# An eight-core decoder-layer kernel: the gating bias moves from TensorE to VectorE, value tiles are tracked one by one, the last normalised writes of a stage move into the next stage, and the last squares go to TensorE directly

## What is computed

```python
def rmsnorm(x, g):
    y = xf * lax.rsqrt(jnp.mean(xf * xf, axis=-1, keepdims=True) + EPS); return y * g
# layer 0
h = rmsnorm(x, norm_mix[0]); z = h @ w_in_even
x = x + concat(pool_mixer(z), conv_mixer(z)) @ w_out_even
x = x + swiglu(rmsnorm(x, norm_ffn[0]))        # (silu(h@Wg) * (h@Wu)) @ Wd, D_FF 2816
# layer 1
z = gelu(rmsnorm(x, norm_mix[1]) @ w_in_odd);  u, v = split(z)
v = rmsnorm(v, g_v)
mixed = einsum('hts,bnshd->bnthd', tril(w_s), chunks_of_128(v)) + b_s   # bias per head and position
x = x + (u * mixed) @ w_out_odd
x = x + swiglu(rmsnorm(x, norm_ffn[1]))
y = rmsnorm(x, norm_final)
```

## Time and profile before

| | |
|---|---|
| median of three runs | 1371.45 us (1371.28 to 1371.82) |
| the profiled execution: its time / its span | 1371.84 us / 1370.3 us (core 2) |
| spans of the eight cores | 1367.2 to 1370.3 us, mean granted clock 0.984 to 0.985 |
| PE busy | 1307.4 us (95%) |
| PEld, DVE, ACT, POOL busy | 721.8, 652.1, 348.3, 214.1 us |

### The profile page before, as it was taken

The page is one execution under the profiler, slowest core; times in us unless marked ns, Lnnn a source line. Parts: engine busy times, 40 slices in busy tenths (PEclk is TensorE's granted clock), DMA queues, the critical chain, the costliest instruction groups (busy, mean ns, idle before and its releaser), DMA issues.

```text
span 1370.3 us, 21873 instructions; the slowest of 8 cores (1367.2 to 1370.3 us)
## 1 busy us (share of the span) xinstructions
PE 1307.4 (95%) x7406; PEld 721.8 (53%) x7406; DVE 652.1 (48%) x1146; ACT 348.3 (25%) x673; POOL 214.1 (16%) x247
## 2 busy tenths in 40 slices
PE   4998997999999999999999999999999999999993
PEld 2554544555555655565444565555565555555552
DVE  3887477223526235632853335822272542644265
ACT  3423342111010110012556324411101011011164
POOL 3200262000000000001821004600000000000076
PEclk9999998999999999999999999999999999999998
DMA  9524203112211223103060101041113111220105
GB/s 264 114 38 63 48 1 62 32 31 54 41 31 32 39 55 62 32 16 61 3 108 1 34 1 32 5 89 32 31 36 58 32 32 31 55 39 16 32 32 217
DMA packets 11048, 68.16 MB, mean 50 GB/s; under 512 B 2056, under 2 KB 2186, under 8 KB 4780
## 3 DMA queue, kind: packets, MB, share of 16 engines
q0 software_dynamic: 6912, 47.19, 19.6%
q1 hardware_dynamic: 3452, 18.95, 3.9%
q10 hardware_dynamic: 576, 0.62, 0.1%
HBM read 105.32 MB, written 9.18 MB: 84 GB/s over the span
## 4 chain that ended last, share of the span: by engine, by line
PE 84%; DVE 7%; issue 4%; POOL 2%; ACT 2%; DMA 1%; DVEq 0%; SPq 0%; ACTq 0%; POOLq 0%
PE bank L741 57%; PE bank L812 16%; PE bank L836 4%; PE bank L1146 2%; PE bank L973 2%; DMA xTs<-xT 1%; POOL sqall L628 1%; DVE R L1168 1%; PE bank L894 1%; DVE hTs L668 1%; DVE R L1088 1%; DVE R L1085 1%; PE bank L1207 0%; PE bank L1199 0%; POOL rsv L1165 0%
## 5 line engine op out<-in xcount | busy, mean ns | idle before, releaser
L741 PE MATMUL bank<-hTs,wring 128*128 128x512 bf16 (+2 forms) x4160 | 737.1, 339 | 12.6 <-DVE mix L794 8.6
L741 PEld LDWEIGHTS bank<-hTs,wring 128*128 128x128 bf16 x4160 | 406.8, 98 | 333.3 <-issue 21.1
L794 DVE TENSOR_TENSOR mix<-bank,gtmp 128x512 bf16<-128x512 f32 (+2 forms) x220 | 129.2, 588 | 472.7 <-PE bank L741 470.4
L749 DVE TENSOR_TENSOR xTs<-bank,xTs 128x512 f32<-128x512 f32 (+2 forms) x480 | 278.9, 587 | 93.8 <-PE bank L741 32.7
L791 ACT ACTIVATE gtmp<-bank 128x512 f32<-128x512 f32 (+2 forms) x220 | 112.8, 515 | 723.5 <-PE bank L741 701.3
L812 PE MATMUL bank<-mix,wring 128*128 128x512 bf16 (+2 forms) x1280 | 224.7, 338 | 0.0
L812 PEld LDWEIGHTS bank<-mix,wring 128*128 128x128 bf16 x1280 | 125.2, 98 | 98.2
L125 POOL DMA_DIRECT2D wring<-wts x46 | 25.0, 543 | 972.0 <-PE bank L741 451.8
L628 POOL TENSOR_TENSOR sqall<-sqall 128x512 f32<-128x512 f32 (+5 forms) x138 | 147.1, 1066 | 95.0 <-ACT sqall L624 82.6
L741 PE MATMUL bank<-mix,wring 128*128 128x512 bf16 (+2 forms) x640 | 113.2, 338 | 0.0
L624 ACT ACTIVATE sqall<-xTs 128x512 f32<-128x512 f32 (+2 forms) x138 | 75.3, 548 | 91.5 <-DVE xTs L749 70.6
(11 more groups left out here) (104 smaller groups left out, 466.1 us busy)
## 6 DMA issues: line engine op xcount, KB each, us to landing
wring<-wts POOLq DMA_DIRECT2D x38, 1024.0 KB, 9.1
xTs<-xT SPq DMA_DIRECT2D x3, 2048.0 KB, 24.1
yT<-xTs SPq DMA_DIRECT2D x3, 2048.0 KB, 6.4
wring<-wts POOLq DMA_DIRECT2D x4, 768.0 KB, 9.3
wring<-wts POOLq DMA_DIRECT2D x4, 512.0 KB, 7.8
mix<-wts POOLq DMA_DIRECT2D x2, 1024.0 KB, 18.6
xTs<-xT SPq DMA_DIRECT2D x1, 1088.0 KB, 34.6
xTs<-xT SPq DMA_DIRECT2D x4, 256.0 KB, 5.2
```

The costliest lines, as they stand in the source:

```text
L741: last = E.matmul(bk[:, 0:w], lhsT=wt[:, o:o + 128], rhs=src_[:, k, c0:c0 + w], start=(k == 0), stop=(k == nk - 1))
L749: sc.op("dve", lambda E: E.tensor_tensor(out=xs(m, n), in0=bk[:, 0:w], in1=xs(m, n), op=ALU.add), reads=[bkB, xB[m][n]], writes=[xB[m][n]])
L794: sc.op("dve", lambda E, bu_=bu_, gi=gi, w=w, c0=c0, slot=slot: E.tensor_tensor(out=mix[:, slot, c0:c0 + w], in0=bu_[:, 0:w], in1=gtmp[gi] ...
```

## The change

1. The bias matmuls of U are gone, with `bs2`, `bs02`, `sel` and their eight DVE operations in `late_setup`. The bias comes repeated over the 128 partitions by one DMA of 512 KB into `bsT` (the space of the squares), issued in V behind tile 1. DVE adds it in PSUM in f32 before its multiplication.
2. `ssB` becomes 17 buffers, one for each token tile.
3. `nm.end()` no longer empties the list, except in the last norm; `last` puts the norm on `active`, and `drip` pops three entries behind each Silu product of `ffn_up`, or two for each token tile of V. `use_banks(8)` comes when the list is empty.
4. The squares of the blocks in `direct` are written by ACT in bf16 into buffers of their own and summed by ones matmuls of their own, for every n: block 7 in the norms behind `out0` and `out1`, blocks 6 and 7 behind both `ffn` (in the last norm this was so for n = 4 alone). The other squares are bf16 too.
5. In the last norm POOL writes only block 7 for n below 4 (it wrote 3 and 7); DVE writes one more.

```diff
@@ late_setup: the eight bias operations on DVE and three small DMAs are removed
-            for (f_, A_, L_, dst_, key) in ((bs_f, bsA, bsL, bs2, "bs_f"), (bs0_f, bs0A, bs0L, bs02, "bs0_f")):
...
+        active = []
+        def drip(k_):
+            if active:
+                active[0].pop(k_)
+                if not active[0].q:
+                    active.pop()
+                    use_banks(8)
@@ Norm.square
-                dr = self.direct if n == 4 else ()
+                dr = self.direct
                 if c in dr:
-                    i = nxt("rng", 2)
+                    i = dr.index(c)
                     sc.op("act", lambda E: E.activation(
-                        out=rngb[i][:, 0:w], in_=xs(c, n), func=AF.Square),
-                        reads=[xB[c][n]], writes=[rngB[i]])
+                        out=drc[i][:, 0:w], in_=xs(c, n), func=AF.Square),
+                        reads=[xB[c][n]], writes=[drcB[i]])
@@ Norm.on_pool, end, last
-                return self.final and c in ((1, 4, 7) if n == 4 else (3, 7))
+                return self.final and c in ((1, 4, 7) if n == 4 else (7,))
             def end(self):
-                self.pop_pool()
-                self.pop(KC)
+                if self.final:
+                    self.pop_pool()
+                    self.pop(KC)
             def last(self):
                 self.mid(4)
-                self.pop_pool()
-                self.pop(KC)
+                if self.final:
+                    self.pop_pool()
+                    self.pop(KC)
+                else:
+                    active.append(self)
@@ ffn_up
-                    if pending:
-                        flush_pending()
-                        use_banks(8)
+                    flush_pending()
...
+                        drip(3)
-        out_proj("out0", Norm(VC_NFFN + 0), out0)
+        out_proj("out0", Norm(VC_NFFN + 0, direct=(7,)), out0)
-        ffn(0, Norm(VC_NMIX + 8))
+        ffn(0, Norm(VC_NMIX + 8, direct=(6, 7)))
-        out_proj("out1", Norm(VC_NFFN + 8))
+        out_proj("out1", Norm(VC_NFFN + 8, direct=(7,)))
@@ V
+            flush_pending()
+            drip(2)
+            if i == 1:
+                sc.dma("sp", bsT, d_bs, writes=bsB_, sem="bsin")
-                reads=vtBs, writes=slotB(0) + [ssB])
+                reads=vtBs, writes=slotB(0) + [ssB[i]])
@@ U
-                    E.matmul(bm[:, 0:pw], lhsT=ones[:, :],
-                             rhs=bs2[:, h * 128:(h + 1) * 128].unsqueeze(1).broadcast_to([128, nq, 128]),
-                             start=True, stop=False)
+                sc.op("dve", lambda E, bm=bm, pw=pw, nq=nq, h=h: E.tensor_tensor(
+                    out=bm[:, 0:pw].rearrange("p (q t) -> p q t", q=nq),
+                    in0=bm[:, 0:pw].rearrange("p (q t) -> p q t", q=nq),
+                    in1=bsT[:, h * 128:(h + 1) * 128].unsqueeze(1).broadcast_to([128, nq, 128]), op=ALU.add),
+                    reads=[bmB] + bsB_, writes=[bmB])
```

More of the change, by code:

```diff
@@ L563, in late_setup @@
                     op0=ALU.mult), reads=[identB, cB["ws00"]], writes=[diagB])
-            selB = Buf("sel")
-            sc.dma("sp", sel[:], d_sel, writes=[selB], sem="cin_sel")
-            for (f_, A_, L_, dst_, key) in ((bs_f, bsA, bsL, bs2, "bs_f"), (bs0_f, bs0A, bs0L, bs02, "bs0_f")):
[L567 to L571, removed]
-                    out=A_, in0=A_, scalar1=sel[:, 0:1], scalar2=None, op0=ALU.mult),
-                    reads=[bsB, selB], writes=[bsB])
-                sc.op("dve", lambda E, A_=A_, L_=L_, dst_=dst_: E.scalar_tensor_tensor(
-                    out=dst_[0:2, :], in0=L_, scalar=sel[:, 1:2], in1=A_, op0=ALU.mult, op1=ALU.add),
-                    reads=[bsB, selB], writes=[bsB])
-            merge(allR1, list(lB.values()) + [bsB])
+            merge(allR1, list(lB.values()))
         warmB = Buf("actwarm")
@@ L1120, in slotB @@
             return [mB[s_][n] for n in range(5)]
-        ssB = Buf("ss")
+        ssB = [Buf(f"ss{i}") for i in range(17)]
+        bsT = sqf[:, 1024:2048]
         nhB = Buf("neghalf")
@@ L1198, in f @@
                 def f(E, bm=bm, h=h, pw=pw, nq=nq, q0=q0, has_s=has_s):
-                    E.matmul(bm[:, 0:pw], lhsT=ones[:, :],
-                             rhs=bs2[:, h * 128:(h + 1) * 128].unsqueeze(1).broadcast_to([128, nq, 128]),
-                             start=True, stop=False)
-                    if has_s:
-                        E.matmul(bm[:, pw:pw + NS], lhsT=ones[:, :], rhs=bs02[:, h * 16:(h + 1) * 16],
-                                 start=False, stop=False)
                     last = None
@@ L1208, in f @@
                                         lhsT=vN3[:, q0 + q, h * 128:(h + 1) * 128],
-                                        rhs=wsT[:, h * 128:(h + 1) * 128], start=False,
-                                        stop=(q == nq - 1 and not has_s))
+                                        rhs=wsT[:, h * 128:(h + 1) * 128], start=True, stop=True)
                     if has_s:
                         last = E.matmul(bm[:, pw:pw + NS], lhsT=vN3[0:16, 16, h * 128:(h + 1) * 128],
-                                        rhs=diag[0:16, h * 16:(h + 1) * 16], start=False, stop=True)
+                                        rhs=diag[0:16, h * 16:(h + 1) * 16], start=True, stop=True)
                     return last
-                rd = [onesB, bsB, wsTB] + [vNB[q0 + q] for q in range(nq)]
+                rd = [wsTB] + [vNB[q0 + q] for q in range(nq)]
                 if has_s:
@@ L1218, in build_program @@
                 sc.op("pe", f, reads=rd, writes=[bmB])
+                sc.op("dve", lambda E, bm=bm, pw=pw, nq=nq, h=h: E.tensor_tensor(
[3 more added lines that the diff above has]
+                    reads=[bmB] + bsB_, writes=[bmB])
+                if has_s:
+                    sc.op("dve", lambda E, bm=bm, pw=pw, h=h: E.tensor_scalar(
+                        out=bm[:, pw:pw + NS], in0=bm[:, pw:pw + NS], scalar1=bsT[:, h * 128:h * 128 + 1],
+                        scalar2=None, op0=ALU.add), reads=[bmB] + bsB_, writes=[bmB])
                 sc.op("dve", lambda E, bm=bm, gi=gi, c0=c0, w=w, h=h: E.tensor_tensor(
```

47 lines of the change are left out of this document (15 added, 32 removed).

## The result

The changed kernel takes 1341.39 us (median of four runs, 1341.04 to 1342.01) against 1371.49 us (1371.28 to 1371.82): a ratio of 0.978, 95% interval 0.976 to 0.980. The forecast was 1342.

What follows compares the result with a forecast made beforehand. PE, holding 84% of the span, was taken as the bound, with time won at its waits, low clock and omissible work. Terms summed to -29.35 from 1371.84 us, giving 1342.5, median 1342; range 1338 to 1346 (chance 0.58).

Steps and rivals of the forecast that it cites:

- Bias off PE, -7.1: In U, dropping the bias matmuls saves PE 0.89 us a head, 7.1 us in all; DVE's additions cost nothing.
- Rival 3: In U, DVE's add and product take over 1.95 us a 512 tile, losing the 7.1: 1349 us; chance 0.08.
- V tile by tile, -6.8: In V, Squares no longer wait for the previous tile's write, so the waiting and low clock at U's start go: -6.8 us.
- The 0.3 and 0.6 allowed beside it: +0.3 us for DVE ending V's last tile at U's start; +0.6 for tile 4's norm ending nearer PE's first value tile.
- The drip, -10.85: Behind `out0`, DVE's first product comes earlier, so PE's 8.55 us wait and 2.3 us of low-clock loss go: -10.85 us.
- Rival 4: Behind `out0`, the first product still comes late and PE keeps its 10.85 us: 1353 us; chance 0.05.
- Squares direct, +0.9, +1.7 - 4.6, +0.9: Extra ones matmuls cost 0.9 in `out0`, 1.7 in `ffn(0)`, 0.9 in `out1`; `ffn(0)`'s wait and low clock go, -4.6 us.
- POOL is the bound there: seven adds of 1.27 us: In `ffn(0)`'s last part, POOL's adds cause PE's 2.93 us wait before tile 3's ones matmul.
- Rival 2: Waits beside the norms are DVE's, not POOL's; direct squares buy nothing in `ffn(0)`, and the last stage's 4.4 stays: 1351; chance 0.09.
- The last stage, -4.4: In the last part of `ffn(1)`, DVE is full from tile 2's first write; the end comes 4.4 us sooner.
- Rival 1: In the last stage DVE keeps up, so the tail is worth 9 us for 4.4: 1337 us; chance 0.15.
- The slower rival: In U, PE waits as long as 2.56 us every head and U runs at 1.2 GHz throughout: 1407 us; chance 0.03.

Runs made afterwards that it cites:

- experiment 3: Changed kernel with U's bias added by ones matmuls on PE again, its rows built by DVE later, behind products of the first ffn: 1348.47 us, +7.1.
- experiment 8: Changed kernel with one more DVE operation, a multiplication by one in PSUM, for each of U's 40 tiles: 1361.52 us, +20.1.
- experiment 2: Changed kernel with one tracked buffer for the value tiles' sums of squares instead of 17: 1348.81 us, +7.4.
- experiment 1: Changed kernel with the late writes again in one piece, without the drip; the eight bias operations stay away: 1345.54 us, +4.2.
- experiment 4: Changed kernel with no direct squares in `ffn(0)`, all eight squares summed by POOL, in bf16: 1343.57 us, +2.2.
- Experiment 9: Changed kernel with one direct square behind the first ffn (block 7) instead of two (blocks 6 and 7): 1342.29 us, +0.9.
- experiment 11: Changed kernel with the last norm's ones matmuls, Ln and Exps placed one block sooner: 1340.26 us, -1.1.

## Why the prediction was right, by its steps

- *Bias off PE, -7.1:* shown by experiment 3 (+7.1) and by heads of 8.09. The cover is thinner than written: DVE has 6.65 us of a head, not 6.0 to 6.5, since the product starts 0.87 after an add of 0.69. Rival 3, U paced by DVE, comes true only once DVE has more than PE's 8.09 a head (experiment 8, with 10.2).
- *V tile by tile, -6.8:* shown by experiment 2 (+7.4). The 0.3 and 0.6 allowed beside it were about right; V and U together gave -12.7 for -13.0.
- *The drip, -10.85:* -11.3. The step put it all down to the drip; experiment 1 splits it into 4.2 for the drip and some 7 for the bias operations that went, with `diag` in it. Rival 4 falls: the first product came at 219.06, before 221. That margin was smaller than written, since `diag` took 4.94 us for the 3.3 of the step.
- *Squares direct, +0.9, +1.7 - 4.6, +0.9:* the sizes were +0.7, -3.2 and +0.8. "POOL is the bound there: seven adds of 1.27 us" was the weakest step. It describes the kernel before, where the adds of tile 3 stand 0.2 to 0.5 us apart; but with adds of 1.16, experiment 4 keeps 2.53 of the 2.93 us although POOL waits for squares. Experiment 9, with block 7 alone direct, leaves 0.42. So at tile 3 the direct squares gain above all by taking away the add behind the last square, not by making POOL's list shorter. By the trace that square is late because DVE is full (5.00 of 5 us busy from 667.3 to 672.3), so that its add comes late; no run tests this. The number of adds counts at tile 4 (experiment 9). The size of the term came out because it rested on the end of square 7, 2 us before PE went on, and not on the count of adds. Rival 2 falls: without direct squares 2.2 us come back.
- *The last stage, -4.4:* -4.5, with the first write of tile 2 and the end 0.1 and 0.2 us from the count. Its chain held: Ln stands on ACT behind squares of the next tile, as the count had it. That the order of the calls made this so, and that 1.1 us could be had by changing it, the step did not see (experiment 11). Rival 1, DVE keeping up, did not come true: DVE ran in pairs of 1.26 from tile 2's first write on.
- *The slower rival:* there is no wait in U, so its condition never arose; experiment 8 did not reach it either.
- *What is left:* the sum was -29.35, the stages gave -31.0. Of the 1.65 between them, 0.65 are in stages that the change does not touch and 0.5 at the drip; the other stages are off by 0.1 to 0.3, V and U the other way. That the median lies only 0.6 from the forecast is in part luck. For the profiled execution, of which the sum was made, 1342.5 stood against 1341.04; the median was taken to lie 0.4 below it, and after the change it lies 0.35 above.
